# The first token group of a hybrid encoder kernel, taken by blocks of the inner dimension for all four token tiles

## The reference

```python
def _chunked_spatial_gating(x, w_in, norm_g, norm_b, w_s, b_s, w_out):
    h = jax.nn.gelu(x @ w_in, approximate=False)      # x 512x1024, w_in 1024x4096
    u, v = jnp.split(h, 2, axis=-1)                   # each 512x2048
    v = _layer_norm(v, norm_g, norm_b)
    ...
```

## Time and profile before

| | |
|---|---|
| three runs of the kernel before | 1295.92, 1297.23, 2141.65 us |
| median | 1297.23 us |
| the profiled execution, own time | 1298.59 us |
| its span, first to last instruction | 1296.9 us |
| mean granted TensorE clock | 0.998 of 2.4 GHz |

### The profile page before, as it was taken

The page is one execution under the profiler, slowest core; times in us unless marked ns, Lnnn a source line. Parts: engine busy times, 40 slices in busy tenths (PEclk is TensorE's granted clock), DMA queues, the critical chain, the costliest instruction groups (busy, mean ns, idle before and its releaser), DMA issues.

```text
span 1296.9 us, 15592 instructions
## 1 busy us (share of the span) xinstructions
PE 1277.5 (99%) x6078; PEld 1051.6 (81%) x6078; DVE 637.2 (49%) x879; ACT 456.9 (35%) x545; POOL 154.6 (12%) x155
## 2 busy tenths in 40 slices
PE   7999999999999999999999999999999999999997
PEld 6788888889888888888888777787888888888886
DVE  3527868356443434433363566664743434343346
ACT  3522334322232323322314577766132323232230
POOL 3002000040000000000315443424200000000001
PEclk9999999999999999999999999999999999999999
DMA  8435932250323232222513334234122232322221
GB/s 271 134 98 134 241 126 86 97 195 1 128 86 103 84 105 84 103 96 94 185 48 99 98 90 122 81 115 141 55 98 97 95 99 90 103 90 102 95 103 65
DMA packets 99771, 140.59 MB, mean 108 GB/s; under 512 B 5200, under 2 KB 76968, under 8 KB 99472
## 3 DMA queue, kind: packets, MB, share of 16 engines
q1 hardware_dynamic: 94304, 127.67, 30.2%
q0 software_dynamic: 5280, 12.07, 3.6%
q10 hardware_dynamic: 144, 0.26, 0.1%
HBM read 137.85 MB, written 10.52 MB: 114 GB/s over the span
## 4 chain that ended last, share of the span: by engine, by line
PE 91%; DVE 4%; DMA 2%; issue 1%; ACT 1%; DVEq 0%; SPq 0%; ACTq 0%
PE bank L1208 30%; PE bank L1211 29%; PE bank L1212 29%; DMA w_raw<-in_a_w_in_dram 2%; PE bank L1570 1%; PE bank L1224 1%; DVE xt_lo L731 1%; PE bank L1594 1%; DVE x_tok L785 1%; DVE w_lo L726 1%; DVE r_stat L754 0%; ACT xt_hi L436 0%; DVE x_tok L748 0%; DVE x_tok L776 0%; PE bank L1430 0%
## 5 line engine op out<-in xcount | busy, mean ns | idle before, releaser
L1208 PE MATMUL bank<-xt_hi,w_hi 128*128 128x512 f32 (+1 forms) x1008 | 383.3, 380 | 1.9 <-DVE w_lo L726 1.5
L1212 PE MATMUL bank<-xt_hi,w_lo 128*128 128x512 f32 (+1 forms) x1008 | 378.9, 376 | 0.0
L1211 PE MATMUL bank<-xt_lo,w_hi 128*128 128x512 f32 (+1 forms) x1008 | 378.8, 376 | 0.0
L726 DVE TENSOR_TENSOR w_lo<-w_raw,w_hi 128x2048 fp32r<-128x2048 f32 x79 | 180.8, 2289 | 194.9 <-ACT w_hi L431 168.6
L1208 PEld LDWEIGHTS bank<-xt_hi,w_hi 128*128 128x128 f32 x1008 | 189.7, 188 | 38.3 <-issue 4.7
L1211 PEld LDWEIGHTS bank<-xt_lo,w_hi 128*128 128x128 f32 x1008 | 189.8, 188 | 34.9 <-issue 1.4
L1212 PEld LDWEIGHTS bank<-xt_hi,w_lo 128*128 128x128 f32 x1008 | 189.7, 188 | 34.8
L431 ACT CAST w_hi<-w_raw 128x2048 fp32r<-128x2048 f32 x53 | 101.3, 1912 | 198.7 <-PE bank L1208 188.4
L1208 PE MATMUL bank<-w_hi,s_hi 128*128 128x512 f32 x416 | 162.6, 391 | 0.0
L1211 PE MATMUL bank<-w_lo,s_hi 128*128 128x512 f32 x416 | 161.9, 389 | 0.0
L1212 PE MATMUL bank<-w_hi,s_lo 128*128 128x512 f32 x416 | 161.9, 389 | 0.0
(11 more groups left out here) (191 smaller groups left out, 1408.4 us busy)
## 6 DMA issues: line engine op xcount, KB each, us to landing
w_raw<-in_f_w_in_dram SPq DMA_DIRECT2D x44, 1024.0 KB, 5.1
w_raw<-in_f_w_down_dram SPq DMA_DIRECT2D x22, 1024.0 KB, 4.8
w_raw<-in_a_w_in_dram SPq DMA_DIRECT2D x14, 1024.0 KB, 5.6
bias_by_query_key<-bias_by_distance POOLq DMA_DIRECT2D x4, 2048.0 KB, 37.1
w_raw<-in_a_w_out_dram SPq DMA_DIRECT2D x8, 1024.0 KB, 4.8
w_raw<-in_b_w_qkv_dram SPq DMA_DIRECT2D x16, 512.0 KB, 5.1
bias_sb<-bias_by_query_key SPq DMA_DIRECT2D x32, 256.0 KB, 2.7
w_raw<-in_b_w_qkv_dram SPq DMA_DIRECT2D x4, 1024.0 KB, 5.2
```

Of the source, the lines that this page charges most:

```text
L726: dve.tensor_tensor(lo_of(u), w_raw[:, u % 2, :], hi_of(u), ALU.subtract).then_inc(w_lo_done, 1)
L1208: ins = pe.matmul(o, a_hi, b_hi, start=start, stop=False)
L1211: pe.matmul(o, a_hi, b_lo, start=False, stop=False)
L1212: return pe.matmul(o, a_lo, b_hi, start=False, stop=stop)
```

## The change

Token tiles are no longer taken one after another in the first group. The inner dimension is: column block k of x (128 of the 1024 columns, all four token tiles) is turned into one PSUM bank, `bank[4 + k % 4]`, cast and split as one 128x512 block, and multiplied with the weight rows of the same k for all four tiles before block k + 2 is turned. x is loaded in five column blocks (of 1, 1, 2, 2 and 2 times 128 columns), which alternate with the six weight pieces. The counts of `xt_hi_done`, `xt_lo_done` and `turned` become 8 in this stage in place of 4, so later waits use `row_count`. `w_used` is raised at the first product of block 4 rather than at the second half of tile 2. POOL's wait is for the fifth x load.

```diff
-            xv = x[0].rearrange("(t p) d -> t p d", p=P)
-            sp.dma_start(x_tok[:, 0, :], xv[0]).then_inc(x_landed[0], 16)
...
+            xk = x[0].rearrange("(t p) d -> p t d", p=P)
+
+            def x_columns(c):
+                k = slice(X_COLS[c][0] * P, X_COLS[c][1] * P)
+                sp.dma_start(x_tok[:, :, k], xk[:, :, k]).then_inc(x_landed[c], 16)
...
+            x_columns(0)
+            first_unit(0)
+            x_columns(1)
+            first_unit(1)
+            x_columns(2)
+            first_unit(2)
+            first_unit(3)
+            x_columns(3)
+            second_unit(0)
+            x_columns(4)
+            second_unit(1)
             load_tokens_side(a_w_in[0], WIDTH, U_AV, N_AV, 2)
...
+            def column(k):
+                act_e.wait_ge(turned, k + 1)
+                act_e.copy(xt_hi[:, k, :], col_bank(k)[:, :]).then_inc(xt_hi_done, 1)
 
             piece(0)
-            first_half(0)
+            column(0)
+            column(1)
             piece(1)
...
+            for k in range(2, 4):
+                column(k)
+                piece(k)
+            column(4)
             piece(4)
+            column(5)
+            column(6)
             piece(5)
...
+            column(7)
...
+            for k in range(4):
+                piece(k)
+                column(k)
             piece(4)
+            column(4)
+            column(5)
             piece(5)
...
+            column(6)
+            column(7)
...
+            def turn_column(k):
+                pe.wait_ge(x_landed[[k0 <= k < k1 for k0, k1 in X_COLS].index(True)], 16)
+                if k == 0:
+                    pe.wait_ge(ident_done, 1)
+                if k >= 4:
+                    pe.wait_ge(xt_lo_done, k - 3)
+                for t in range(TB):
+                    ins = pe.transpose(col_bank(k)[:, t * P:t * P + P], x_tok[:, t, k * P:k * P + P], ident[:, :])
+                ins.then_inc(turned, 1)
...
+                hi_ready()
+                if last:
+                    pe.wait_ge(xt_lo_done, k + 1)
+                    for t in range(TB):
+                        hi_hi(t)
+                        hi_lo(t)
+                        lo_hi(t).then_inc(v_mm, 1)
+                    return
+                for t in range(TB):
+                    ins = hi_hi(t)
+                    if k == 4 and t == 0:
+                        ins.then_inc(w_used, 1)
+                w_lo_ready()
+                for t in range(TB):
+                    hi_lo(t)
+                pe.wait_ge(xt_lo_done, k + 1)
+                for t in range(TB):
+                    lo_hi(t)
+
+            turn_column(0)
+            turn_column(1)
+            for k in range(KD):
+                column_product(k)
+                if k + 2 < KD:
+                    turn_column(k + 2)
...
-            pool.wait_ge(x_landed[3], 16)
+            pool.wait_ge(x_landed[4], 16)
```

More of the change, by code:

```diff
@@ L277, in rows_of, with col_bank, row_count @@
             return s_hi[:, j % 2, :, :], s_lo[:, j % 2, :, :]
-        def turn_bank(e, t):
-            return 4 + 2 * (t % 2) if e == 0 else 2 * t
+        def col_bank(k):
+            return bank[4 + k % 4]
+        def row_count(e, t):
+            return KD + TB * (e - 1) + t + 1
+        X_COLS = [(0, 1), (1, 2), (2, 4), (4, 6), (6, 8)]
         def gate_rows(m):
@@ L833, in piece, with column @@
                 ins.then_inc(w_lo_done if p in (3, 5) else piece_lo, 1)
[L835 to L847, removed]
+            def column(k):
+                dve.wait_ge(xt_hi_done, k + 1)
+                dve.tensor_tensor(xt_lo[:, k, :], col_bank(k)[:, :], xt_hi[:, k, :], ALU.subtract
+                                  ).then_inc(xt_lo_done, 1)
+            for k in range(4):
+                piece(k)
+                column(k)
             piece(4)
+            column(4)
+            column(5)
             piece(5)
-            for t in range(2, TB):
-                split_rows(0, t)
+            column(6)
+            column(7)
             def group_stats(g):
@@ L1214, in turn @@
             def turn(e, t):
[L1216 to L1222, removed]
+                pe.wait_ge(rows_ready, TB * (e - 1) + t + 1)
                 for k in range(KD):
-                    ins = pe.transpose(bank[turn_bank(e, t) + k // 4][:, k % 4 * P:k % 4 * P + P],
+                    ins = pe.transpose(bank[2 * t + k // 4][:, k % 4 * P:k % 4 * P + P],
                                        x_tok[:, t, k * P:k * P + P], ident[:, :])
-                    if e == 0 and t == 0 and k == KD // 2 - 1:
-                        ins.then_inc(half_turned, 1)
-                    if k == 0 and t == 0 and e > 0:
+                    if k == 0 and t == 0:
                         ins.then_inc(w_used, 1)
@@ L1362, in _ @@
[L1362 to L1375, removed]
@@ new lines, in column_product, with hi_ready, w_lo_ready, hi_hi @@
+            def column_product(k):
+                u, kk = k // 4, k % 4
+                w = slice(kk * NB, kk * NB + NB)
+                last = k == KD - 1
+                def hi_ready():
+                    pe.wait_ge(xt_hi_done, k + 1)
+                    if k < 3:
+                        pe.wait_ge(piece_hi, k + 1)
+                    elif k == 4:
+                        pe.wait_ge(piece_hi, 4)
+                    elif k in (3, 6):
+                        pe.wait_ge(w_hi_done, u + 1)
+                def w_lo_ready():
+                    if k < 3:
+                        pe.wait_ge(piece_lo, k + 1)
+                    elif k == 4:
+                        pe.wait_ge(piece_lo, 4)
+                    elif k in (3, 6):
+                        unit_ready(u)
+                def hi_hi(t):
+                    return pe.matmul(bank[t][:, :], xt_hi[:, k, t * P:t * P + P], w_hi[:, u, w], start=k == 0, stop=False)
+                def hi_lo(t):
+                    return pe.matmul(bank[t][:, :], xt_hi[:, k, t * P:t * P + P], w_lo[:, u, w], start=False, stop=False)
+                def lo_hi(t):
+                    return pe.matmul(bank[t][:, :], xt_lo[:, k, t * P:t * P + P], w_hi[:, u, w], start=False, stop=last)
+                hi_ready()
[16 more added lines that the diff above has]
+                    lo_hi(t)
```

67 lines of the change are left out of this document (12 added, 55 removed).

## The result

The changed kernel takes 1299.98 us in the median of 11 runs (1298.84 to 1303.34); the kernel before, run beside it, 1297.23 (from 1293.73). The ratio is 1.0028 with a 95% interval of 1.0017 to 1.0039: slower by 2 to 5 us. The ratios further down leave out one execution of the kernel before of 2141.65 us and one with the broadcasts later of 2596.9 us, without which their medians are 1296.58 and 1296.41. The forecast was 1293.7 with a range to 1297.4. The profiled execution took 1299.8 us, with a span of 1298.1.

What follows compares the result with a forecast made beforehand. TensorE, busy for 99% of the span, was taken to bound the kernel. A start shorter by 4.2 us and a stall of 0.7 gave -3.5 us, from 1297.2 to 1293.7, range 1290.8 to 1297.4.

Steps and rivals of the forecast that it cites:

- what is moved later: Unit 3's load, issued at 27.5, collides with POOL's broadcast loads from about 26.3; it must land by 36.8.
- I take 10.0 ... a stall of 0.7 us: Unit 3's load takes 10.0 us from issue to landing, so TensorE waits 0.7 us at line 1393.
- Rival A: Unit 3 takes 12.5 us to land, line 1393 waits 3.2 us more: -1.0, 1296.2 us; chance 0.19.
- The landmark's gain: Start of line 1380, after the first group's products and transposes: 33.4 us in place of 37.57, 4.2 us less.
- the clock's rise: TensorE's faster clock in the first group comes at 11.3 us, bounds 9.5 and 14.5, worth +0.9 and -1.6 us.
- carried to the end: Later program is unchanged, so what the start and first half of group 1 win or lose lasts to the end.
- The loads: At the start, x's first block lands at 3.9 us, first weight piece 4.6, second column block 5.2; later loads run ahead.
- one of the prediction's own signs of being wrong: In the first group, a wait of the turns for x loads would show the forecast wrong; no size given.
- the estimate by it, 8.9 us: Unit 3's load sharing engines by turns with POOL's queue takes 8.9 us in all; the sum would be -4.2.
- B: At the start, clock rises no earlier or blocks come late: landmark 35.9, no stall, -1.7, 1295.5 us; chance 0.14.
- C: Unit 3 lands 25.7 us after 27.5, TensorE waits 12.2 us: 1305.2 us; decides past 15 us; chance 0.05.
- D: Wait for x and weights was hidden anyway or returns at another wait of group 1: 1297.2 us; chance 0.04.

Runs made afterwards that it cites:

- the broadcasts later: Changed kernel, with POOL's three broadcast loads waiting until ACT has cast unit 3, not unit 1: 1296.68 us, ratio 0.9989; the same edit on the kernel before: 1296.42 us, 1.0002.
- The kernels without the wait: Changed kernel with one-hot rows first (0.9983), that plus piece 5 cast early (0.9985), POOL's broadcasts delayed, piece 5 early, or that plus block 1 turned later (0.9989 each).
- the turn inside: Changed kernel with piece 5 cast early and block 1 turned behind the second four products of block 0: 1294.42 us, ratio 0.9989.
- the wait made: Kernel before, with two extra DVE subtractions between unit 3's cast and its low part, so TensorE waits at line 1393: 1303.12 us, ratio 1.0045.

## Why the prediction was wrong

**The step that failed** is the one under what is moved later: "I take 10.0 ... a stall of 0.7 us". Its mechanism held in each part: POOL's loads and unit 3 collided, the chain from the cast to the one-hot rows took 48.04 - 39.48 = 8.6 us, TensorE would have come to line 1424 at 45.8, forecast 45.4. Two sizes were off. Unit 3 was issued at 28.1 for 27.5 and took 11.3 us for 10.0, so the wait was 2.28 us for 0.7. The part missing altogether was what a wait does to the clock: I priced each microsecond of it at one and gave no reason. The wait of 2.28 us cost 2.28 + 1.70 + 1.5, 2.4 for each, and the same in the second profile: 2.24 of wait and 3.2 at the lower level. Rival A had the place, with a wait of 3.2 us, and ended below before all the same, since it too priced a microsecond at one.

**The landmark's gain** came out as 3.8 us against the one profile, forecast 4.2; but about 2.0 over four profiles of the old order and eight of the new. I had taken one profile for the kernel. Both the hole at 9.60 and the pace up to 13 us vary from run to run. The profile had the longest hole of the four, 1.80 us where the others have 0.8 us or less, and the second latest rise of the clock. That 33.80 came so near to the forecast 33.4 was in part luck: the products started 1.5 us late, but only 2.75 us of them ran at the lower level, up to 10.47, for 5.1 in the sum, which gives 1.2 back. The prediction used the clock's rise as a term and gave it bounds for the new order only.

**With these sizes the sum comes out.** In the mean of the two profiles of the changed kernel the wait is 2.3 us and the lower level 3.2. -2.0 + 2.3 + 3.2 = +3.5 us, and the measured ratio gives +3.6. The kernels without the wait should be 2.0 us ahead, 0.9985; they are at 0.9983, 0.9985 and three times 0.9989.

**What is won at the start is not all carried to the end**, as the prediction took it. Near 168 us the four profiles of the old order wait 1.48, 0.43, 0.32 us and not at all; eight of nine of the new order wait 0.95 to 2.86 us there, and only the second of the changed kernel doesn't. I matched the profiles product by product against the first one. Coming out of that place, the four of the old order have gained 0, 1.1, 1.2 and 1.5 us on it, 0.9 in the mean; the four of the new order whose clock fell nowhere have gained 0.0 to 0.5 us, 0.2 in the mean. So in these profiles about 0.7 of the 2.0 us is lost again there, and more where the clock falls. The cause is open.

**The loads.** Column block 0 landed about when forecast (turns from 3.70, forecast 3.9). Block 1 took 5.0 us from its issue at 1.90 and landed at 6.9, forecast 5.2: a wait of the turns of 2.14 us, where the sum had a few tenths, and one of the prediction's own signs of being wrong. Its price was small: with the turn inside the wait is gone, and the ws turns began no earlier than without. The later blocks came in time, as forecast, and so did ACT and DVE: TensorE has no gap from 7.72 to 45.6.

**The queues.** The Trainium skill (DMA: Bandwidth & Descriptors, Queues, rings and completion order) has the engines take turns between queues; the estimate by it, 8.9 us, is too low here. The traces have 11.3 and 11.5 us with the first of POOL's loads 1 us ahead, 12.1 with it 0.2 ahead, 8.6 with it 1.5 behind, 7.3 with it 1.7 behind, and 5.4 alone. That the two share agrees, the size does not.

**The other rivals.** B had the late block, but no late clock. C did not come: the load took 11.3 us, under the 15 from which it was to decide. Those sizes were wrong even by the prediction's own terms. With 9.3 us to land in and 4.2 us to lose, the load decides at 13.5 us; and for C, 8.6 us of chain behind a landing at 53.2 make the one-hot rows ready at 61.8, a wait of 16.4 us and not 12.2. The measured point lies far lower still, since with the clock's fall a wait of 2.28 us cost 5.5, and the gain was 2.0. D, no change, fell: the kernel is slower.

## What to carry to other kernels

When a step is moved later, look at what is queued behind it on each engine that does not need it: two instructions of DVE, 2.0 us long, stood behind a load that they don't use, and cost the kernel 5.5 us; moving them alone was enough. Price a wait of the engine that bounds the kernel with the clock that it may lose, not by its length. And before forecasting from the first microseconds of one profile, ask how much they vary: here one profile's start was 1.1 us off the mean of its order, more than half of what the change could win.

## What the runs showed of the hardware

Waits of TensorE in full work behind which the granted clock stayed: 0.95, 0.97, 1.22, 1.48, 1.49 and 1.51 us. Waits behind which it fell: 1.72, 1.90, 2.16, 2.16, 2.19 and 2.86 us. It then stayed down for 3.4 or 6.8 us, and products of 512 columns started 0.43 us apart in place of 0.23. I had priced waits of this length at their length alone. In the two profiles of the changed kernel the fall cost 3.2 us beside the wait, in the old order with the wait made 1.55 us, where the clock was down for half as long.

The clock column of the windows shows 1.00 up to the first rise even where the pace is that of 1.2 GHz; it is of use only from there on.
